# Full attention: 64 stationary value columns that alternate between the halves of the output partitions, weights summed on GpSimd

## What is computed

```python
def axial_gqa_attention(q, k, v, q_g, k_g, tables):
    ...
    def one_block(q_blk):
        s = jnp.einsum('bkgqd,bksd->bkgqs', q_blk, kt).astype(jnp.float32) * scale
        p = jax.nn.softmax(s, axis=-1).astype(vt.dtype)
        return jnp.einsum('bkgqs,bksd->bkgqd', p, vt)
    ...
```

## Time and profile before

| | |
|---|---|
| median of 3 runs | 1996.31 us (1996.07 to 1999.24) |
| profiled execution, span | 1999.4 us |
| PE, DVE, ACT, POOL busy in it | 96%, 60%, 45%, 5% |
| the attention that is changed | first values 280.5, the stage after it starts at 521.6 us |

### The profile page before, as it was taken

One profiled execution on the slowest core, in us unless ns is written; L12 is line 12 of the kernel. 1 busy time (PEld: TensorE's weight loads), 2 busy tenths in 40 slices (PEclk: granted clock), 3 DMA queues, 4 the chain that ended last, 5 costly groups with the idle time before them and its releaser, 6 DMA issues.

```text
span 1999.4 us, 23686 instructions
## 1 busy us (share of the span) xinstructions
PE 1928.1 (96%) x8844; PEld 1507.4 (75%) x8844; DVE 1209.4 (60%) x1774; ACT 909.3 (45%) x1523; POOL 104.6 (5%) x188
## 2 busy tenths in 40 slices
PE   6999999999989989999999999999999999999888
PEld 4778876656787768888888788887888887776577
DVE  7794847655575687677555546556543555445744
ACT  5543345465553542333333435434523665445742
POOL 1101100000000000111000000000021000000000
PEclk9999999999999999999999999999999999999999
DMA  8437400010205423355221653333432001013062
GB/s 325 161 95 241 165 25 11 1 53 1 95 1 167 160 95 121 138 184 200 68 70 53 219 202 121 120 127 138 158 126 74 33 32 43 22 56 146 1 179 95
DMA packets 67151, 216.13 MB, mean 108 GB/s; under 512 B 8272, under 2 KB 13520, under 8 KB 66784
## 3 DMA queue, kind: packets, MB, share of 16 engines
q1 hardware_dynamic: 47168, 141.15, 21.1%
q0 software_dynamic: 19872, 73.48, 10.4%
HBM read 177.30 MB, written 34.61 MB: 106 GB/s over the span
## 4 chain that ended last, share of the span: by engine, by line
PE 57%; DVE 4%; ACT 2%; DMA 2%; issue 1%; DVEq 0%; SPq 0%; ACTq 0%
PE ps L1216 9%; PE ps L1218 8%; PE ps L1217 8%; PE ps L1522 6%; PE ps L1523 6%; PE ps L1524 6%; PE ps L1366 4%; DMA w_raw<-in_weights 2%; PE ps L1342 1%; PE ps L1344 1%; PE ps L1310 1%; DVE w_lo L2158 1%; PE ps L1652 1%; PE ps L1651 1%; PE ps L1650 1%
## 5 line engine op out<-in xcount | busy, mean ns | idle before, releaser
L1216 PE MATMUL ps<-h_hi,w_hi 128*128 128x512 f32 x832 | 335.5, 403 | 7.5 <-DVE h_lo L2158 5.2
L1218 PE MATMUL ps<-h_hi,w_lo 128*128 128x512 f32 x832 | 326.4, 392 | 0.0
L1217 PE MATMUL ps<-h_lo,w_hi 128*128 128x512 f32 x832 | 326.1, 392 | 0.0
L2158 DVE TENSOR_TENSOR w_lo<-w_raw,w_hi 128x1024 fp32r<-128x1024 f32 x139 | 170.0, 1224 | 244.0 <-ACT w_hi L1689 242.6
L1689 ACT ACTIVATE w_hi<-w_raw 128x1024 fp32r<-128x1024 f32 x140 | 147.6, 1056 | 243.6 <-DMA w_raw<-in_weights 241.8
L2290 DVE TENSOR_REDUCE mh<-ps 128x1 f32<-128x512 f32 (+1 forms) x224 | 140.2, 630 | 142.1 <-PE ps L1307 68.0
L1216 PEld LDWEIGHTS ps<-h_hi,w_hi 128*128 128x128 f32 x832 | 158.1, 190 | 43.1 <-DVE h_lo L2158 6.4
L1218 PEld LDWEIGHTS ps<-h_hi,w_lo 128*128 128x128 f32 x832 | 157.3, 189 | 34.1
L1217 PEld LDWEIGHTS ps<-h_lo,w_hi 128*128 128x128 f32 x832 | 157.7, 190 | 32.1 <-issue 1.4
L1216 PE MATMUL ps<-hid_hi,w_hi 128*128 128x512 f32 x352 | 138.1, 392 | 4.1 <-DVE hid_kept_lo L2158 1.9
L1522 PE MATMUL ps<-t_hi,pair_S_r 128*128 128x512 f32 x352 | 137.3, 390 | 4.4 <-DVE pair_S_r L2158 2.6
(11 more groups left out here) (405 smaller groups left out, 3829.9 us busy)
## 6 DMA issues: line engine op xcount, KB each, us to landing
w_raw<-in_weights SPq DMA_DIRECT2D x140, 512.0 KB, 3.6
ada_next<-in_ada POOLq DMA_DIRECT2D x32, 512.0 KB, 4.8
ada_last<-in_ada POOLq DMA_DIRECT2D x24, 512.0 KB, 5.2
pair_gate<-in_weights SPq DMA_DIRECT2D x22, 512.0 KB, 3.7
pair_up<-in_weights SPq DMA_DIRECT2D x22, 512.0 KB, 4.6
ada_first<-in_ada SPq DMA_DIRECT2D x8, 1024.0 KB, 17.7
m_scratch<-y POOLq DMA_DIRECT2D x12, 512.0 KB, 5.5
hid_scratch<-hid_out POOLq DMA_DIRECT2D x22, 256.0 KB, 2.3
```

The lines of the kernel that those rows point to most:

```text
L1216: e.matmul(o, w_hi[slot][:, tile_of(kw)], hi, start=start, stop=False, skip_group_check=skip)
L1217: e.matmul(o, w_hi[slot][:, tile_of(kw)], lo, start=False, stop=False, skip_group_check=skip)
L1218: return e.matmul(o, w_lo[slot][:, tile_of(kw)], hi, start=False, stop=stop, skip_group_check=skip)
L2158: return e.tensor_tensor(dst, src, hi.bitcast(F32), ALU.subtract)
```

## The change

In "full" attention the stationary operand of the values shrinks to the 64 value columns, so that a product writes 64 output partitions. Units with an even number write partitions 0 to 63 of the job's bank and the odd ones 64 to 127. The values of four units are issued in a row, in units 0 (the last four of the job before) and 4 (the first four of this job), behind the maximum product; the last four of the last job come at the end. The weight tiles become seven (an eighth stands in for one of them later on), so that exponentials can run ahead.

The sums of the weights no longer come out of the value product. GpSimd adds the weight tiles of a job, one by one, into `p_sums` (`psum`, 7 adds of 128x512 per job). In unit 2 of the next job PE multiplies ones by that tile (`dsum`), into an auxiliary bank; the bank is free when ACT has taken the logarithm. `take` comes in unit 3 and `div` in unit 4. The division multiplies both halves of the output by the reciprocals and adds them, three instructions where one was.

Semaphores are merged to make room: `qk_n`, `qk_swap`, `qk_sin`, `qk_cos` become `qk_step`, and `ln_r` becomes part of `inv`. The ones beside the values are no longer written by ACT, and the row of ones beside the keys is written in two halves.

```diff
@@ -211,10 +214,26 @@
         for step in rows + waiting + others + slots.get(g, []):
             p.add(*step)
         waiting = [("div", *x[1:]) for x in waiting if x[0] == "take"]
+        if job[0] == "full":
+            if u:
+                p.add("psum", *job, u)
+            if g and u % V_GROUP == 0:
+                for i1, u1 in units[g - V_GROUP:g]:
+                    p.add("val", *jobs[i1], u1)
+            if i and u == 2:
+                p.add("dsum", *jobs[i - 1])
+                waiting.append(("take", *jobs[i - 1]))
+            other(share(job))
+            continue
         other(share(job))
         p.add("val", *job, u)
         if u == len(units_of(*job)) - 1:
             waiting.append(("take", *job))
+    if jobs[-1][0] == "full":
+        for i1, u1 in units[-V_GROUP:]:
+            p.add("val", *jobs[i1], u1)
+        p.add("dsum", *jobs[-1])
+        waiting = [("take", *jobs[-1])]
     while fill:
         for step in fill.pop(0):
             p.add(*step)
...
@@ -821,18 +840,18 @@
-                self.v = [v_area[i](f"{n}_v{i}", [P, KT, P], F32) for i in range(2)]
+                self.v = [v_area[i](f"{n}_v{i}", [P, KT, 64 if n == "full" else P], F32) for i in range(2)]
-        A1 = Buffers("full", four(64, 72, 80, 88), four(68, 136), area, (76, 92, 144))
+        A1 = Buffers("full", four(64, 72, 80, 88), four(68, 136), area, (76, 92, 144, 94, 146, 78, 70, 112))
-        area = Area(148, 152)
-        A1.rinv = [area(f"rinv1_{i}", [64, HT], F32) for i in range(2)]
+        A1.rinv = [Area(148, 150)("rinv1", [P, HT], F32)] * 2
+        A1.sums = [Area(start, start + 2)(f"p_sums{i}", [P, HT], F32) for i, start in enumerate((138, 150))]
...
@@ -1042,6 +1061,8 @@
+            if AUX[i][0] == "dsum":
+                return s["inv"], 2 * no(*AUX[i]) - 1
...
@@ -1074,9 +1095,22 @@
                 c += q1 - q0
             return found
 
+        FULL_P = 7
+
+        def weights_at(kind, i):
+
+            if kind != "full":
+                return AB[kind].pf[(i - 1) % 3]
+            last = no("val", "full", 3, 1, KT - 1)
+            return A1.pf[7 if i > last and (i - 1) % FULL_P == 6 else (i - 1) % FULL_P]
+
         def score_cols(kind, h, n, u):
             found = columns_of(kind, h, n, u)
             return found[0][3], found[-1][3] + found[-1][2] - found[-1][1]
+
+        def summed(i):
+
+            return (KT - 1) * ((i - 1) // KT) + max((i - 1) % KT, 1)
 
         def q_ready(kind, h, n):
 
...
@@ -1361,11 +1395,21 @@
                         e.wait_ge(s["sink_l"], no("mrow", kind, h, n) - 16)
                         e.matmul(ps[:, bank, :], one_row[0:97, :], sink_h[job % 2][0:97, :], start=True, stop=False,
                                  skip_group_check=True).then_inc(s["sink_mm"], 1)
+                if kind == "full":
+                    e.matmul(ps[rows_of(u), bank, :], A.v[kb][:, u, :], weights[:, :], start=u < 2, stop=u >= KT - 2,
+                             skip_group_check=True).then_inc(s["val"], 1)
+                    return
                 for kt, q0, q1, c in columns_of(kind, h, n, u):
                     o = ps[:, bank, q0 - n * HT:q1 - n * HT]
-                    x = e.matmul(o, A.v[kb][:, kt, :], A.pf[p3][:, c:c + q1 - q0], start=(u == 0 and kind != "band"), stop=False,
+                    x = e.matmul(o, A.v[kb][:, kt, :], weights[:, c:c + q1 - q0], start=(u == 0 and kind != "band"), stop=False,
                                  skip_group_check=True)
                 x.then_inc(s["val"], 1)
+
+            def weight_sums(kind, h, n):
+                aux_free(("dsum", kind, h, n))
+                e.wait_ge(s["p_sum"], no("psum", kind, h, n, KT - 1))
+                e.matmul(ps[:, aux_bank("dsum", kind, h, n), :], ones[:, :], A1.sums[job_no(kind, h, n) % 2][:, :], start=True, stop=True,
+                         skip_group_check=True).then_inc(s["den_mm"], 1)
 
             def gate(part):
                 if part in G_COLS:
...
@@ -1773,9 +1817,9 @@
-                copy(A1.v[i][:, :, 64:P], ones[:, 0:64].unsqueeze(1).to_broadcast([P, KT, 64])).then_inc(s["at_set"], 1)
-                copy(A1.ka[i][64:65, :].rearrange("p (a b) -> p a b", a=KT),
-                     ones[64:65, :].unsqueeze(1).to_broadcast([1, KT, P])).then_inc(s["at_set"], 1)
+                for half in range(2):
+                    copy(A1.ka[i][64:65, half_of(half)].rearrange("p (a b) -> p a b", a=4),
+                         ones[64:65, :].unsqueeze(1).to_broadcast([1, 4, P])).then_inc(s["at_set"], 1)
...
@@ -1820,22 +1864,32 @@
             def scores(kind, h, n, u):
                 A, i = AB[kind], no("sc", kind, h, n, u)
                 c0, c1 = score_cols(kind, h, n, u)
-                p3, bank = (i - 1) % 3, 2 + i % 2
+                bank, weights = 2 + i % 2, weights_at(kind, i)
                 e.wait_ge(s["sc"], i)
-                if i > 3:
+                if kind == "full":
+                    if i > FULL_P:
+                        e.wait_ge(s["val"], i - FULL_P)
+                        e.wait_ge(s["p_sum"], summed(i - FULL_P))
+                    else:
+                        e.wait_ge(s["m_kept"], kept(QM + 3, QM + 7, OM + 3))
+                else:
                     e.wait_ge(s["val"], i - 3)
-                else:
-                    e.wait_ge(s["m_kept"], kept(QM + 3, QM + 7, OM + 3))
-                e.activation(A.pf[p3][:, c0:c1], ps[:, bank, c0:c1], ACT.Exp, scale=SC).then_inc(s["p_exp"], 1)
+                e.activation(weights[:, c0:c1], ps[:, bank, c0:c1], ACT.Exp, scale=SC).then_inc(s["p_exp"], 1)
 
             def take(kind, h, n):
                 job = job_no(kind, h, n)
                 rinv, bank = AB[kind].rinv[job % 2], 6 + job % 2
-                e.wait_ge(s["val"], no("val", kind, h, n, last_unit((kind, h, n))))
-                if job >= 2:
-                    e.wait_ge(s["div"], job - 1)
-                e.activation(rinv[:, :], ps[64:P, bank, :], ACT.Ln).then_inc(s["ln_r"], 1)
-                e.wait_ge(s["ln_r"], job + 1)
+                if kind == "full":
+                    e.wait_ge(s["den_mm"], no("dsum", kind, h, n))
+                    if job >= 1:
+                        e.wait_ge(s["div"], job)
+                    e.activation(rinv[:, :], ps[:, aux_bank("dsum", kind, h, n), :], ACT.Ln).then_inc(s["inv"], 1)
+                else:
+                    e.wait_ge(s["val"], no("val", kind, h, n, last_unit((kind, h, n))))
+                    if job >= 2:
+                        e.wait_ge(s["div"], job - 1)
+                    e.activation(rinv[:, :], ps[64:P, bank, :], ACT.Ln).then_inc(s["inv"], 1)
+                e.wait_ge(s["inv"], 2 * job + 1)
                 e.activation(rinv[:, :], rinv[:, :], ACT.Exp, scale=-1.0).then_inc(s["inv"], 1)
 
             def gate(part):
...
@@ -2226,17 +2280,16 @@
-                e.scalar_tensor_tensor(x, y[:, QA + t, :], col("qk_g", t), q_sq[r % 2][:, :], ALU.mult, ALU.mult).then_inc(s["qk_n"], 1)
-                e.wait_ge(s["qk_n"], r + 1)
-                e.stream_shuffle(z, x, [(i + 16) % 32 for i in range(32)]).then_inc(s["qk_swap"], 1)
-                e.wait_ge(s["qk_swap"], r + 1)
+                e.scalar_tensor_tensor(x, y[:, QA + t, :], col("qk_g", t), q_sq[r % 2][:, :], ALU.mult, ALU.mult).then_inc(s["qk_step"], 1)
+                e.wait_ge(s["qk_step"], 4 * r + 1)
+                e.stream_shuffle(z, x, [(i + 16) % 32 for i in range(32)]).then_inc(s["qk_step"], 1)
+                e.wait_ge(s["qk_step"], 4 * r + 2)
-                tt(z, z, sin1[:, :], ALU.mult).then_inc(s["qk_sin"], 1)
-                tt(x, x, cos1[:, :], ALU.mult).then_inc(s["qk_cos"], 1)
+                tt(z, z, sin1[:, :], ALU.mult).then_inc(s["qk_step"], 1)
+                tt(x, x, cos1[:, :], ALU.mult).then_inc(s["qk_step"], 1)
-                e.wait_ge(s["qk_sin"], r + 1)
-                e.wait_ge(s["qk_cos"], r + 1)
+                e.wait_ge(s["qk_step"], 4 * r + 4)
...
@@ -2306,7 +2359,16 @@
 
             def divide(kind, h, n):
                 job = job_no(kind, h, n)
-                e.wait_ge(s["inv"], job + 1)
+                e.wait_ge(s["inv"], 2 * job + 2)
+                if kind == "full":
+                    out, rinv, r = q_src(kind, h, n), A1.rinv[0], half_rows(h)
+                    e.wait_ge(s["val"], no("val", kind, h, n, KT - 1))
+                    tt(out, ps[0:64, 6 + job % 2, :], rinv[0:64, :], ALU.mult).then_inc(s["div_part"], 1)
+                    e.wait_ge(s["div_part"], 2 * job + 1)
+                    tt(rinv[r, :], ps[64:P, 6 + job % 2, :], rinv[64:P, :], ALU.mult).then_inc(s["div_part"], 1)
+                    e.wait_ge(s["div_part"], 2 * job + 2)
+                    tt(out, out, rinv[r, :], ALU.add).then_inc(s["div"], 1)
+                    return
                 tt(q_src(kind, h, n), ps[0:64, 6 + job % 2, :], AB[kind].rinv[job % 2][:, :], ALU.mult).then_inc(s["div"], 1)
 
```

(12 more changed lines are left out.)

15 lines of the change are left out of this document (8 added, 7 removed).

## The result

The changed kernel took **2043.5 us** (median of 4 runs, 2041.5 to 2046.7) beside 1997.6 for the kernel before on the same chip: ratio 1.0227, 95% interval 1.0214 to 1.0241. It is 46 us slower. The forecast was 2003 with a range of 1976 to 2032: the sign was right, the size was not.

What follows compares the result with a forecast made beforehand. PE's own queue order was taken to pace the first attention. Job waits +2.7, last job -0.5, stage end +3.1 and scans +1.5 gave +6.8 on 1999.4, so 2006.2, less 3 for the median: 2003 us, range 1976 to 2032.

Steps and rivals of the forecast that it cites:

- The sum 2.7 - 0.5 + 3.1 + 1.5 = +6.8: First attention: job waits left uncovered, last job, stage end, then gate scans with ACT steps; +6.8 us in all.
- rival 2: DVE steps with two SBUF inputs and GpSimd adds hold each other up: +12 to +38, 2015 us; chance 0.23.
- PE's order bounds the stage: First attention before the change: PE is full, 20.00 of 20 us at clock 1.00, and its queue order sets the pace.
- Groups of 2.35: Four half-column values on PE: 2.15 us with overlapping halves plus 0.2 for switching shape, 2.35 per group.
- Adds of 1.2, dsum of 0.86, nothing waits for GpSimd: Per job, seven GpSimd adds of 1.2 us fit inside the job; PE's summing product takes 0.86.
- The end of the stage: From last exponential to memory stage: 6.4 us instead of 3.2, for adds, dsum, logarithm, reciprocal and division; +3.1.
- The walk: One job without other work, followed through the queues: 2.4 us of PE waits, 13.7 us against 12.98, +0.7 per job.
- Rival 1: ACT and DVE answer in time and PE still bounds the stage: jobs of 11.6 us, -19, 1977 us; chance 0.18.
- Rival 3: The column halves do not overlap, so each value group takes 3.64 us: +41, 2044 us; chance 0.11.
- Rival 4: GpSimd's adds pace the jobs, from 1.95 us an add; at 4 us, +240, 2240 us; chance 0.06.

Runs made afterwards that it cites:

- a1: Changed kernel with GpSimd adding only 8 of 512 columns from the third job on, so sums are wrong; 2016.2 us, ratio 1.0091.
- f2: Changed kernel with 8-column GpSimd adds from job 2 and six filling products before the wait for each row of maxima; 2014.6 us, ratio 1.0078.
- a4: Kernel before, values and order untouched, with seven 128x512 GpSimd adds per job on scratch tiles; 2013.7 us, ratio 1.0075.
- a2: Changed kernel with values in groups of two units instead of four, GpSimd adds whole; 2048.1 us, ratio 1.0243.
- b2: Changed kernel with logarithm and reciprocal a unit earlier, in unit 2, and the division in unit 3; 2032.4 us, ratio 1.0164.
- c2: Changed kernel with the tiny maximum and the division's third step rewritten to read one SBUF input, GpSimd adds whole; 2024.0 us, ratio 1.0120.
- e1: Changed kernel with six unused 512-column products on PE before the row of maxima in 15 of 16 jobs; 2026.1 us, ratio 1.0136.
- f1: Changed kernel with early logarithm and reciprocal, one-SBUF-input forms and six filling products together; 2015.4 us, ratio 1.0084.
- f5: Changed kernel with early logarithm, one-input forms, values moved to the expected waits, and six filling products; 2051.9 us, ratio 1.0264.
- f3: Changed kernel with early logarithm, one-input forms and values moved to the expected waits, no filling; 2032.2 us, ratio 1.0165.

## Why the prediction was wrong in size

The steps that failed are two. The sum 2.7 - 0.5 + 3.1 + 1.5 = +6.8 takes VectorE's steps beside running adds at the lengths they have without them, so it puts the hold-up of rival 2 at nothing; measured, it is 11 to 14 us. And it prices every wait of PE at its own length and all work at full clock, so the lower clock, the largest part with 25 to 30 us, has no term in it or in any rival. Point by point, in the order of the prediction.

- **PE's order bounds the stage**: right as a reading of before. What it left out is that a PE at 20.00 of 20 us was also what held its clock.
- **Groups of 2.35**: the term was oversized; 1.87 was measured. The forecast let each unit wait for the first half of the one before; the trace has no such wait, and the switch costs about 0.15 for entering and leaving together, not 0.2. This made the forecast 32 x 0.48 = 15 us too long in PE's time, but PE's time was not the bound, so little of it shows.
- **Adds of 1.2, dsum of 0.86, nothing waits for GpSimd**: adds 1.35. dsum waits for them 2.3 us in all, and that is the last job: 4.35 us for the last three adds. The end of the stage was given as 6.4 from the last exponential; by the rows it is 564.59 - 556.08 = 8.5 (the exponentials at 555.00 take 1.08). With narrow adds (a1) it is 5.8.
- **The walk**: its three waits are there. In a1, job without other work, idle times of 0.47 at the maximum of unit 4 (on the logarithm), 0.66 at the row of maxima and 0.41 at the next scores. Idle begins behind modelled ends that lie 0.17 after the streaming (0.40 against 0.23), so they are 0.64, 0.83 and 0.58, together 2.05 where the walk has 0.81 + 0.66 + 0.65 = 2.12. The rows of one such job:

```profile
411.20 0.47 PE L1376 MATMUL ps<-full_qq,full_kk 128*128 128x512 f32 x1 [0.41 <-ACT full_qa L1853]
...
419.14 0.50 PE L1341 MATMUL ps<-full_kk,full_qq 128*128 128x512 f32 x1 [0.47 <-ACT rinv L1886]
...
423.54 0.40 PE L1357 MATMUL ps<-ident_r,mx 128*1 128x128 f32 x4 [0.66 <-DVE mh L2343]
```

The job is 13.48 against 13.7. **The order alone**: a1 less its clock sum is 2016.2 - 14.0 = 2002.2, f2 less filling and clock sum 2014.6 - 12.2 - 1.7 = 2000.7, where the kernel before, measured beside them, took 1998.6 and 1999.8: +1 to +4. The walk's total, +6.8, was for this part a little high, and its 2003 is close to the time that the kernel would have without the two costs that follow.
- **Rival 2, the step that failed first**: the forecast gave the hold-up nothing and the rival a chance of 0.23, with 2015. It happens in every job, at the two places the rival named and at others (`full_qa`, the cast, the scans). The size comes out three ways. In a4's trace, at full clock, the stage ends 12.2 us later. A job without other work takes 14.21 in the changed kernel and 13.48 in a1, so 16 x 0.73 = 12. And a1 against after, less the difference of the two clock sums and the 2.7 at the end of the stage, gives 27.3 - 11.2 - 2.7 = 13. The rival's price, 12, was good, its chance was too low: GpSimd's seven adds run 7 x 1.35 = 9.4 of the 14.2 us of a job, and of the two steps one had only to begin in them. "If every one meets it" was nearly the case.
- **What no part had: the clock.** 25 us by the clock sum, 30 by the table below. Together: 1998 + 1 to 4 (order) + 3 (end of the stage) + 12 (hold-up) + 25 to 30 (clock) = 2039 to 2047, where 2043.5 was measured. That this closes proves little: the order was taken as what is left of a1 and f2 without the clock, and only a4 prices its part independently. The clock is the largest part, and the bound by which I widened my range did not know of it, as each stall was priced once. The causes are not independent: the clock falls because of pauses, and the pauses come from order and hold-up. The Trainium skill, "TensorE: Matmul & The Clock Gate", section "A second HAM failure mode: psum-queue depth-cycling", tells of a kernel in which short idle times between groups of matmuls make the clock swing and cost throughput; the 25 us of the clock sum point the same way.
- **Rival 1** (1977) did not happen: even at full clock and without the hold-up the kernel is at 2001 to 2002 (estimates from f2 and a1). **Rival 3** gave 2044 and the median is 2043.5, by accident: the rows show starts that overlap, and the real one-half kernel is at 2075. **Rival 4** needed adds of 1.95; they take 1.35. (By its own numbers, 16 x (28 - 13.7) = 229, its time is 2232 and not 2240.)

The clock can be priced a second way, without windows. Each execution comes with the mean clock of its whole span, and time x (1 - clock) is an estimate of what it lost. Executions of one kernel bear it out: a2 took 2041.4 at 0.985 and 2050.1 at 0.980, and less the lost time both come to 2009 to 2011. Means over the executions of a kernel, in us; the clock is known to 0.001, so the last two columns to about 1 us:

| kernel | time | lost to the clock | the rest |
|---|---|---|---|
| before (beside a1 to a4) | 1998 | 11 | 1987 |
| after | 2044 | 41 | 2003 |
| a1, narrow adds | 2016 | 27 | 1989 |
| a4, before with adds | 2013 | 12 | 2001 |
| b2, early logarithm | 2033 | 41 | 1992 |
| c2, one input in SBUF | 2024 | 27 | 1997 |
| e1, filling | 2027 | 15 | 2012 |

So the clock costs 41 - 11 = 30 of 46 us. The rest grows by 16: about 2 for the order (a1 against before) and 14 for the adds (after against a1, the end of the stage with 3 among them); a4 has 14 for the hold-up. Filling gives 26 us of clock back and costs 9, and the early logarithm gains nothing from the clock.

What stays open: why the same pause is followed by a low clock in one job and not in another, and how the lost clock divides between the order and the hold-up, since both make pauses. No kernel here beats the kernel before; the best form of the changed one is at +0.8% (f1).

## What to carry to other kernels

Where an engine was full and a change leaves short pauses in it, price each pause twice: its own length, and the slower clock of the work that may follow it. If GpSimd gets elementwise work beside a chain of short VectorE steps, look at those with two inputs in SBUF, however tiny; a 128x4 maximum took 0.70 us instead of 0.16, and one-input forms took the cost away at once. And a time that agrees with a rival proves no rival: the length of one group in the trace does.

## What the runs showed that was not expected

- Full-precision products in 64 stationary columns, alternating between both halves of the output partitions, overlap fully: 1.87 us for four of 512 columns, 3.58 in one half.
- Six useless products per job made the kernel 17 us faster (e1), and 20 us slower where little pause stood at their place (f5 against f3).
- GpSimd is held up as well: an add that meets two such DVE steps (at 468.14 above) took 2.23 us, against 1.28 alone.
- The clock was lower behind a pause, not in it: 0.50 to 0.57 in windows in which PE is full, 1.00 in the window with 0.70 of 3 us busy.
